# A two-layer diffusion step with expert retrieval: consumers of a dense step read it at a later lookup than its producer

## The reference

```
h  = rms_norm(x, norm1_g) * (1 + sc1) + sh1
qa, ka, va, qb, kb, vb, ci, cb, cc = split(h @ w_in)          # 1024 -> 2560 columns
oa = attention(rms_norm(qa), rms_norm(ka), va)                 # 6 heads
ob = attention with two softmax maps, p1 - lam * p2            # 6 heads
oc = cb * conv3(cc * ci)
x  = x + g1 * (concat(norm(oa), norm(ob), norm(oc)) @ w_out)
h  = rms_norm(x, norm2_g) * (1 + sc2) + sh2
q  = h @ peer_wq;  scores = q . sub_keys                       # 8 heads x 2 halves x 128 keys
16 best pairs of keys for each head -> 16 of 16384 experts for each token and head
x  = x + g2 * sum_k gate_k * gelu(u_k . h) * v_k               # u_k, v_k gathered from HBM
```

## Time and profile before

| | us |
|---|---|
| median of 3 runs | 2656.48 |
| lowest and highest run | 2642.13, 2659.6 |
| the profiled execution: device time | 2647.17 |
| the profiled execution: span | 2645.3 |

### The profile page before, as it was taken

One profiled execution on the slowest core, in us unless ns is written; L12 is line 12 of the kernel. 1 busy time (PEld: TensorE's weight loads), 2 busy tenths in 40 slices (PEclk: granted clock), 3 DMA queues, 4 the chain that ended last, 5 costly groups with the idle time before them and its releaser, 6 DMA issues.

```text
span 2645.3 us, 23982 instructions
## 1 busy us (share of the span) xinstructions
PE 1826.4 (69%) x6452; PEld 728.3 (28%) x6452; DVE 1636.9 (62%) x4145; ACT 1161.7 (44%) x3776; POOL 899.1 (34%) x773
## 2 busy tenths in 40 slices
PE   6876967887577665575665598788768655555555
PEld 2344324434143221122331133433424211111111
DVE  1335557755656566676656558785566676667764
ACT  1215315534455344544444544564444444444443
POOL 0002213222434334433334323232344544444543
PEclk9878978788788877777887799879879877778777
DMA  9958999677989999988999989787999999989997
GB/s 360 387 199 346 369 375 352 257 276 284 420 344 418 401 413 393 419 309 354 415 415 417 364 314 368 264 308 279 372 381 393 421 419 415 417 359 421 421 418 310
DMA packets 188440, 963.35 MB, mean 364 GB/s; under 512 B 15993, under 2 KB 18425, under 8 KB 89233
## 3 DMA queue, kind: packets, MB, share of 16 engines
q0 software_dynamic: 110592, 805.36, 75.2%
q1 hardware_dynamic: 77712, 156.47, 16.1%
HBM read 959.15 MB, written 2.62 MB: 364 GB/s over the span
## 4 chain that ended last, share of the span: by engine, by line
PE 32%; DMA 31%; DVE 16%; ACT 10%; issue 7%; POOL 3%; SPq 0%; DVEq 0%; POOLq 0%; ACTq 0%
DMA ring<-peer_uv,rows 25%; PE ps_acc L902 13%; DVE ring L1429 7%; PE ps_mm L737 6%; POOL ring L654 3%; PE ps_mm L882 3%; PE ps_mm L854 3%; ACT poly L1077 2%; DMA ring<-ada_w 2%; ACT diags L1086 2%; ACT coef L1081 1%; DMA weights<-w_in 1%; DMA weights<-ada_w 1%; DMA weights<-peer_wq 1%; PE ps_mm L794 1%
## 5 line engine op out<-in xcount | busy, mean ns | idle before, releaser
L654 POOL DMA_INDIRECT ring<-peer_uv,rows x768 | 897.1, 1168 | 1717.9 <-PE ps_acc L902 1295.5
L902 PE MATMUL ps_acc<-ring,diags 128*64 128x512 f32 x3072 | 974.8, 770 | 520.9 <-ACT diags L1086 517.2
L1429 DVE CUSTOM_DVE_ANT_0 ring<-ring,h_twice 128x1024 f32<-128x1024 f32 x768 | 939.1, 1225 | 570.0 <-DMA ring<-peer_uv,rows 517.3
L902 PEld LDWEIGHTS ps_acc<-ring,diags 128*64 128x64 f32 x3072 | 226.2, 163 | 1153.4 <-ACT diags L1086 783.4
L1074 ACT ACTIVATE poly<-dots 128x2 f32<-128x2 f32 x384 | 77.8, 203 | 901.4 <-DVE gated L1437 900.4
L1077 ACT ACTIVATE poly<-poly,dots 128x1 f32<-128x1 f32 x768 | 255.3, 379 | 12.7
L1081 ACT ACTIVATE coef<-poly,gated 128x1 f32<-128x1 f32 x768 | 255.2, 379 | 12.7
L1086 ACT ACTIVATE diags<-consts,coef 128x64 f32<-128x64 f32 x768 | 225.3, 340 | 12.4
L882 PE MATMUL ps_mm<-hT,weights 128*128 128x128 f32 (+1 forms) x1024 | 203.0, 357 | 30.1 <-issue 25.2
L737 PE MATMUL ps_mm<-weights,hT 128*128 128x512 f32 x432 | 198.3, 613 | 13.2 <-DMA weights<-w_in 12.1
L882 PEld LDWEIGHTS ps_mm<-hT,weights 128*128 128x128 f32 x1024 | 171.3, 210 | 95.0 <-issue 73.4
(11 more groups left out here) (183 smaller groups left out, 1581.3 us busy)
## 6 DMA issues: line engine op xcount, KB each, us to landing
weights<-w_in SPq DMA_DIRECT2D x17, 2048.0 KB, 17.9
weights<-peer_wq SPq DMA_DIRECT2D x16, 2048.0 KB, 19.3
weights<-ada_w SPq DMA_DIRECT2D x14, 2048.0 KB, 13.0
ring<-ada_w SPq DMA_DIRECT2D x10, 2048.0 KB, 17.5
ring<-peer_uv,rows POOLq DMA_INDIRECT x768, 10.1
weights<-w_out SPq DMA_DIRECT2D x6, 2048.0 KB, 25.4
ring<-w_in SPq DMA_DIRECT2D x3, 2048.0 KB, 19.4
ring<-w_out SPq DMA_DIRECT2D x2, 2048.0 KB, 16.9
```

The lines of the kernel that those rows point to most:

```text
L654: pool.indirect_dma_start(ring[:, n % SLOTS, :], None, peer_uv1 if n >= PICKS // 2 else peer_uv0, bass.IndirectOffsetOnAxis(ap=picks, axis ...
L902: last = pe.matmul(ps_acc[HALF * j:HALF * (j + 1), b * NB:(b + 1) * NB], diags[:, (n + j) % DIAGS, :], ring[:, (n + j) % SLOTS, DM + b * N ...
L1429: dve.tensor_tensor_reduce(row, row, h_twice[:, half, :], GELU_B, 0.0, ALU.mult, ALU.add, of_head(dots, n)).then_inc(u_used, 1)
```

## The change

Two new step kinds come in, and the code that consumes a result moves to a later step.

- *norm*: the steps are now `pre`, one `norm` for each tile, `post`. ACT's squares and root and PE's first broadcasts are in `pre`; DVE makes h of tile j in the `norm` of j; PE's transposes and ACT's copy of tile j are in the step after it. In the first norm, the second tile's h goes into `scratch`, the first's into `merged`.
- *proj*: ACT copies projection i-1 at step i, for the first three chunks; the last two chunks as before.
- *merge*: a step between `last` and `tile`, which holds DVE's normalisation and ACT's root; PE's transposes and ACT's copy follow in `tile`.
- *out*: ACT copies and DVE mixes output i-1 at step i, and the last one in the norm's `pre`.
- *keys*: PE waits for `keys_ready` before the first key scores, no longer before the first query step.
- *modulation*: on DVE alone (`late=True`), the additions of a step's modulation run at the start of the next step.
- *weights*: one `norm` of 9 (sample) becomes `pre` 5, `norm` 6 for each tile, `post` 4; `merge` has 4. For the prompt 10 becomes 6 + 5 + 4, and `merge` has 4.

```
-WEIGHTS = {False: dict(norm=9, proj=8, ...
+WEIGHTS = {False: dict(pre=5, norm=6, post=4, merge=4, proj=8, ...
+    normed = ["pre"] + ["norm"] * nt + ["post"]
...
+    def late_program(stage):
+        last = ()
+        steps_of = dense_stages(*stage)
+        for at in range(len(steps(stage[1]))):
+            for which in last:
+                modulate(which)
+            next(steps_of)
+            last = PLAN.get(stage, {}).get(at, ())
+            yield
...
 PE, norm
+                broadcasts(0)
+                yield "pre"
+                for j in range(len(tiles)):
+                    if j:
+                        broadcasts(j)
+                        transposes(j - 1)
+                    yield "norm"
+                transposes(len(tiles) - 1)
+                yield "post"
...
                     yield "last"
+                    yield "merge"
                     pe.wait_ge(merged_ready, nth(l, tiles, 1, j))
...
-                pe.wait_ge(keys_ready, group_nth(l, tiles))
                 yield "qk"
                 def half_scores(i):
+                    if i == 0:
+                        pe.wait_ge(keys_ready, group_nth(l, tiles))
...
 ACT
+                for i in range(IN_CHUNKS * nt):
+                    if 0 < i <= QK_CHUNKS * nt:
+                        copy_projection(i - 1)
+                    yield "proj"
+                    if i >= QK_CHUNKS * nt:
+                        copy_projection(i)
...
+                for i in range(OUT_CHUNKS * nt):
+                    if i:
+                        copy_output(i - 1)
                     yield "out"
+                copy_output(OUT_CHUNKS * nt - 1)
...
 DVE
+                for i in range(OUT_CHUNKS * nt):
+                    if i:
+                        mix_output(i - 1)
                     yield "out"
+                mix_output(OUT_CHUNKS * nt - 1)
                 yield from norm(l, tiles, 1)
...
-            programs = stage_programs(modulate, dense_stages)
+            programs = stage_programs(modulate, dense_stages, late=True)
```

More of the change, by code:

```diff
@@ L69 @@
 QK_BESIDE = QK_PARTS // (IN_CHUNKS - QK_CHUNKS)
-WEIGHTS = {False: dict(norm=9, proj=8, late_proj=4, qk=2.5, keys_t=1.5, tile=6, head=4.2, last=2, out=10, pq=7),
-           True: dict(norm=10, proj=9, late_proj=9, qk=3, keys_t=3, tile=8, head=7, last=2, out=9, pq=5)}
+WEIGHTS = {False: dict(pre=5, norm=6, post=4, merge=4, proj=8, late_proj=4, qk=2.5, keys_t=1.5, tile=6, head=4.2, last=2, out=10, pq=7),
+           True: dict(pre=6, norm=5, post=4, merge=4, proj=9, late_proj=9, qk=3, keys_t=3, tile=8, head=7, last=2, out=9, pq=5)}
 def steps(tiles):
     nt = len(tiles)
-    kinds = ["norm"] * nt
+    normed = ["pre"] + ["norm"] * nt + ["post"]
+    kinds = list(normed)
     kinds += ["proj"] * (QK_CHUNKS * nt)
@@ L82, in steps @@
     kinds += ["keys_t"] * (1 if tiles == P_TILES else 3)
-    kinds += (["tile"] + ["head"] * HEADS + ["last", "tile"]) * nt
-    return kinds + ["out"] * (OUT_CHUNKS * nt) + ["norm"] * nt + ["qk"] + ["pq"] * 16
+    kinds += (["tile"] + ["head"] * HEADS + ["last", "merge", "tile"]) * nt
+    return kinds + ["out"] * (OUT_CHUNKS * nt) + normed + ["qk"] + ["pq"] * 16
 FIRST_PQ = 2 * AHEAD + 1
@@ L228, in chunks @@
             found += [(out + 3 * nt, 0, [("keys", l, tiles)])]
-            found += [(out + 3 * nt + 1 + 4 * n, 0, [("q", l, tiles, n)]) for n in range(Q_CHUNKS)]
+            found += [(out + 3 * nt + 3 + 4 * n, 0, [("q", l, tiles, n)]) for n in range(Q_CHUNKS)]
             found += [(at, 1, made) for at, made in PLAN.get((l, tiles), {}).items()]
@@ L406, in build, with normed @@
         transposed = ps_tr
+        def normed(j):
+            return scratch[:, 0:DM] if j else merged[:]
         def keys_at(j):
@@ L941, in norm @@
                 act.activation(rstd[:, 0:nt], sumsq[:, 0:nt], ACT.Sqrt, bias=eps, scale=1.0 / DM).then_inc(rms_root, 1)
[L942 to L946, removed]
+                yield "pre"
+                for j in range(nt + 1):
+                    if j:
+                        act.wait_ge(h_mm, nth(l, tiles, 2, stage * nt + j - 1))
+                        act.activation(hT[:, :, (j - 1) * P:j * P], transposed[:].rearrange("p (k n) -> p k n", k=KC),
+                                       ACT.Copy).then_inc(hT_ready, 1)
+                    yield "norm" if j < nt else "post"
             def dense_stages(l, tiles):
@@ L1030, in dense_stages, with copy_output @@
                     yield "tile"
-                for i in range(OUT_CHUNKS * nt):
+                def copy_output(i):
                     act.wait_ge(out_mm, nth(l, tiles, OUT_CHUNKS, i))
@@ L1349, in dense_stages, with mix_output @@
                                              op0=ALU.mult, op1=ALU.mult).then_inc(merged_ready, 1)
+                    yield "merge"
                     yield "tile"
-                for i in range(OUT_CHUNKS * nt):
+                def mix_output(i):
                     n, t = i // nt, tiles[i % nt]
```

50 lines of the change are left out of this document (25 added, 25 removed).

## The result

The changed kernel took 2610.55 us (median of 4 runs, 2609.15 to 2614.31) against 2655.01 for the kernel before (the median of four runs, one more than ahead of the prediction): a ratio of 0.9842, 95% interval 0.9806 to 0.9879. Run once more, as `e15_after_again`, it took 2610.42 against 2648.54, ratio 0.9863 (0.9843 to 0.9883); 35 to 45 us less were expected of it. By the two ratios the change is worth 36 to 42 us, by the medians 38 to 44; 43 were forecast, and 2606 us for the metric. Its profiled execution took 2611.43 us against 2647.17 before, which is 36 us less.

The account below looks back on a forecast made before the run. Gathers were taken to bound the bare loop, PE most steps of S0 and S1. Terms 2 + 18 + 9 + 3 + 4 + 2 + 8 - 3 = 43 us off 2647.2 gave 2604.2, metric 2606; range 2575 to 2650.

Parts of the forecast that it names:

- What bounds the stretches: Gathers bound the bare loop at 420 GB/s; in S0 and S1 an edit is worth the PE idle time it removes.
- P1's end: End of P1: waits for merge, h and keys, 17.8 us in all, count about half: 8 us gained (0 to 18).
- Second norm, S0: S0's second norm with keys: 18.7 us of PE waits go, small new waits come, clock gives 2.5: 18 us (9 to 21).
- The keys: PE's wait before the first query step goes: 8.03 us in S0; S1's 3.44 is lost again at a weight chunk.
- S1: the first norm and the merges: S1's first norm gains 4 us (0 to 5); of the merges only its second gains, 2 us (0 to 4).
- Projection and output: Late copies and mixing in projection and output steps: PE is never idle for them, so 0 us gained.
- Merge: Of six merge waits totalling 31.9 us, only S1's second gains, by an add before its tile: 2 us (0 to 4).
- The modulation: DVE's sums one step later; weight chunks hold PE in picks 34 to 38 anyway: cost 3 us (0 to 8).
- The third: Rival, chance 0.07: freed ACT and DVE keep the ring fuller, removing more PE idle time in S0 and S1: 2570 us.
- The first: Rival, chance 0.16: PE's idle time goes, but weights come late or DVE becomes the limit: 2640 us.
- The second: Rival, chance 0.08: PE waits 4 us for late copies at each of 22 projection and output steps: 2692 us.
- The likeliest case: The forecast itself, chance 0.69: 43 us less, 2606 us for the metric, its own range 2580 to 2635.

Follow-up runs that it names:

- e15_after_again: The changed kernel run once more, with no further edit, against the kernel before: 2610.42 against 2648.54 us, ratio 0.9863.
- run 38: Not a run label: "38 to 46" is the us expected from norm and keys alone on the kernel before; that run measured 2624.3 us, ratio 0.9933.
- e6_old_projout: The changed kernel with projection and output as before; late norm, merge, keys and modulation stay: 2619.44 us, ratio 0.9893.
- e1_keys: The kernel before, with PE waiting for the copied keys before the first key scores, no longer before the first query step: 2645.93 against 2643.16 us, ratio 1.0009.
- e4_no_merge: The changed kernel without the merge step and its weight; the normalisation stands in the second tile step as before: 2621.53 us, ratio 0.9931.
- e14_no_merge_keys_first: The changed kernel without the merge step, and with ACT's copy of the keys ahead of the second norm's squares: 2614.05 us, ratio 0.9866.
- e10_after_keys_first: The changed kernel with ACT's copy of the keys ahead of the second norm's squares: 2599.68 us, ratio 0.9813.
- e12_keys_first_merge7: The changed kernel with the keys copied ahead of the squares and the sample's merge weight at 7, not 4: 2601.38 us, ratio 0.9829.

## Why the prediction was right, and where its steps were not

The direction, the size and most of the reading of the profile held; the shares of the parts did not. By parts:

| part | forecast, us | measured, us |
|---|---|---|
| norm and keys, alone on the kernel before | 44, by the expectation for its run 38 to 46 | 18 |
| projection and output | 0 | 9 alone; 9 when taken back, less sure |
| merge | 2 | 10 when taken back |
| modulation on DVE | -3 | 0 when taken back |
| all | 43 | 36 to 42 by the ratios |

**What bounds the stretches: right.** The bare loop kept 420 GB/s, and the gain lies in S0, at P1's end and in S1, where PE's idle time fell. By the starts of the same pick's dot in the two profiled executions, 2.6 us were gained before the loop, 14.6 in S0, about 9 in P1 and 7 in S1. The forecast had 2 for the start, 18 for S0 (21 less 3 for the modulation), 8 and 15. Cut at PE's adds, the two second norms gained 20 and 12 us, and P1's end (picks 270 to 352) 7, where 18, 9 and 8 were forecast. What fell short lies elsewhere: picks 0 to 38 took 190.0 us and not 185.1, with PE 28.0 us and not 20.1 at chunks of `ada_w` in S0, and picks 352 to 458, with S1's first norm and merges, took 3 us longer where 6 less were forecast.

The Trainium skill's rule on the most contended engine (Perfetto Trace Analysis, Identifying the Most-Contended Engine), read over the whole span, would have had no gain. The bare loop agrees, with 420 GB/s before and 419 after; the whole kernel does not, as it moves the same 963 MB in 36 us less.

**Second norm, S0: right in place, with other small terms.** The 9.31, the 1.39 and the 8.03 went. I allowed 1.4 for hT and 1.5 for the last mixing; they were 3.18 and 0.27, and 1.98 for the query chunk, which I had not. That PE does not wait for the first tile's h either is thanks to the late output, which I had at nothing: without it (`e6_old_projout`) the mixing is also 0.27, but 4.66 us stand at the second tile's broadcasts. The clock, at 2.5 us given back, was about right: 3 us.

**The keys: right in the whole, wrong as a part by themselves.** I saw for S1 that its second query chunk was issued at the copy of the keys, and set the 3.4 us there against the gain. For S0 I did not, as no wait stood there before, and counted 8.03 in full. `e1_keys` shows 10.61 us of wait for this very chunk in S0. It came in time before only because it took 9.5 us while PE stood, and 26.01 once PE's adds went on. The term missing was that a wait of PE also holds the gathers back, beside which a chunk's transfer is fast. What made the copy come early in the changed kernel is the norm: the chunk was issued at 616.63, at 625.44 before. In S1 it was issued at 1833.21, so the 3.4 us that I took off for it were not lost either: PE waits 0.67 us there.

**S1: the first norm and the merges oversized.** The second norm gained 12 us where I had 9. For the first norm I had 4. The wait of 3.86 us at the transposes is now one of 3.96 at the second tile's broadcasts, as these ask for the first tile's h:

```profile
1496.05 1.12 PE L692 MATMUL ps_mb<-mods,consts 128*128 128x512 f32 x2 [3.96 <-DVE merged L1231]
```

I had priced PE's wait in `pre` and at the transposes, but not `h_ready` ahead of `broadcasts(j)`. In the second norm the wait for the last mixing was 4.43 us where I had 1.5, with the slow clock behind it (3.44 us for the broadcast's first four matmuls, 1.98 before). Over the kernel the waits for hT are the term most undersized: 2.7 us in the sum, 11.6 measured.

**Projection and output: wrong as a zero.** The step was "they end when PE has finished, and PE does not wait for them". That is so in the step itself. What I left out is that an engine that stood in a step is late for the next one: the 6.3 us between mixing and squares in the earlier trace rows, which I read as the cost of the norm's order, were in fact the dots and diagonals that ACT and DVE had not done while they stood in the output step. Two parts of the change work on this one wait, so their prices can't be added.

**Merge: undersized.** By the picks I found one merge of the sample's four with a gain, and that is the one which changed (7.52 to 2.56; the two first ones kept 6.17 and 6.16). The 2 us counted the cover by the add, and it was 5. By the rows of `e4_no_merge` and `e14_no_merge_keys_first` the rest lies at the second norms and at PE's waits for hT, and was not foreseen. Single profiles do not agree on the place: cut at PE's adds, `e4_no_merge` loses 17 us in picks 38 to 102 and none in 420 to 486, and `e14_no_merge_keys_first` 8 and 11 against `e10_after_keys_first`. Why the step is worth 10 us stays open.

**The modulation and P1's end** went about as said: `ada_w` chunks held PE in S0, and the order on DVE made no difference (3 us of cost were forecast); P1's end gained 7 to 8 us, near half of the 17.8, and the half was a guess that came true.

**The rivals.** The third (more, since ACT and DVE are freed) named the mechanism that the projection's runs showed, though the total did not become larger. The first did not come in the changed kernel, but its mechanism did in `e1_keys`: PE's idle time went to late weights, whose transfers take longer as gathers move faster. The second did not come: PE has no wait for a late copy of a projection. It does wait for mixed outputs, 12.7 us, but once in a norm and not in each step. The likeliest case was right in its time partly by luck: an oversized norm and keys and undersized merge, projection and output cancel.

**Slips in the numbers.** DVE was 63% busy in S0 (262.03 of 418 us), not 65%. Half of 17.8 is 9, not 8. The lower bounds of the terms add up to 6 us, so their range reaches to 2641 us, not 2635. None of these moves the forecast by more than 1 us.

The fastest version of the study is `e10_after_keys_first`: the changed kernel with the keys copied ahead of the squares, 2599.68 us, 1.9% under the kernel before and 8 to 13 us under the changed one. `e12_keys_first_merge7` is its equal.

## What to carry to other kernels

Before counting a wait as gained, ask what is issued when the waiting instruction or its producer is done: here a weight chunk's transfer hung on the same copy, and the wait moved there whole until the copy itself was moved. Ask too what the wait held back: a standing PE also kept the gathers off the chunk's way. An engine's wait that costs nothing in its own step can be the reason for its lateness in the next, so price a stall together with what its engines were doing just before. Where several edits shorten one wait, take each away from the whole as well as adding it alone, and see that what is taken away stands where it stood: 18 us added alone and 33 taken away do not settle the norm's worth, as the empty steps also moved its work by two picks.

## What was not expected of the hardware

The granted clock of PE can differ between executions over the same instructions: in picks 38 to 56 it was 0.86 in one profile and 0.76 in another (0.88 and 0.70 in the rows of 409 to 459), with nearly the same waits of PE, and about 7 us between them. In the kernel before a transfer of 2 MB for a query chunk took 8.6 us from issue to landing at 587.19, with 1 MB of gathers beside it, and 30.05 us at 1860.21, with 9.6 MB beside it. So its lead has to be set for the busy case.
